# Seven weight chunks' low halves moved from VectorE to GpSimd in the first mixer of a three-layer network

## The reference

```python
def _mixer(u, w_in, ...):
    proj = u @ w_in
    rq, rk, rv, rg, a_cq, a_ckv, a_kr, a_gret, a_gmla = jnp.split(proj, SPLIT_IDX, axis=-1)
    ...
    y_ret = _head_group_norm(_bidir_retention(rq, rk, rv, decay_f, decay_b), gn_w)
    y_ret = (jax.nn.silu(rg) * y_ret) @ w_ret_out
    c_q = _rmsnorm(a_cq, q_norm_w)
    q = (c_q @ w_uq).reshape(B, L, MLA_HEADS, MLA_QK)
    ...
    y_mla = _mla_attention(q_nope, q_rope, k_nope, k_rope, v).reshape(...) @ w_mla_out
    merged = jax.nn.sigmoid(a_gret) * y_ret + jax.nn.sigmoid(a_gmla) * y_mla
    return merged @ w_o
```

## Time and profile before

| | us |
|---|---|
| median of three runs | 1189.4 |
| profiled execution, its own time | 1190.88 |
| span of the profiled execution | 1189.1 |
| TensorE matmul busy | 1128.5 (95% of the span) |
| VectorE busy | 770.1 (65%) |
| ScalarE busy | 514.3 (43%) |
| GpSimd busy | 6.0 (1%) |

### The profile page before, as it was taken

How to read it: one execution, slowest core, us unless ns; L and a number is a source line. 1 busy time by engine, 2 the same in 40 slices (tenths; PEclk the granted TensorE clock), 3 DMA queues, 4 the chain that set the end, 5 groups by cost and what they waited for, 6 DMA issues and landing times.

```text
span 1189.1 us, 21009 instructions
## 1 busy us (share of the span) xinstructions
PE 1128.5 (95%) x8640; PEld 1069.2 (90%) x8640; DVE 770.1 (65%) x860; ACT 514.3 (43%) x512; POOL 6.0 (1%) x6
## 2 busy tenths in 40 slices
PE   8998999799899999998998999999987999999998
PEld 7996777588889999997887999999987999999998
DVE  5765778576756666677755565655479776655563
ACT  5322443334444444446475543333454455434331
POOL 0000001000000000000000000000000000000000
PEclk8998999799999999999998999999989999999999
DMA  9552135034435575672632456554243534554630
GB/s 314 184 159 90 40 115 169 5 121 146 127 105 161 175 208 163 201 239 85 200 107 71 142 181 209 165 188 152 96 150 108 169 107 151 203 192 165 208 106 36
DMA packets 160886, 175.72 MB, mean 148 GB/s; under 512 B 4512, under 2 KB 146848, under 8 KB 160704
## 3 DMA queue, kind: packets, MB, share of 16 engines
q1 hardware_dynamic: 160544, 174.74, 46.3%
q10 hardware_dynamic: 288, 0.21, 0.1%
HBM read 173.89 MB, written 1.05 MB: 147 GB/s over the span
## 4 chain that ended last, share of the span: by engine, by line
PE 76%; DVE 14%; ACT 6%; issue 2%; DMA 0%; SPq 0%; DVEq 0%; ACTq 0%
PE proj L401 46%; PE aux L759 20%; DVE wlo L1373 5%; DVE f L1376 4%; DVE f L1373 2%; ACT whi L1016 2%; PE aux L458 2%; DVE f L1379 1%; PE aux L686 1%; PE aux L669 1%; PE aux L562 1%; PE aux L556 1%; PE aux L679 1%; DMA f<-in_x_dram 0%; DVE x_all L1373 0%
## 5 line engine op out<-in xcount | busy, mean ns | idle before, releaser
L401 PE MATMUL proj<-u,whi 128*128 128x256 f32 (+1 forms) x2912 | 538.3, 286 | 12.5 <-DVE wlo L1373 4.1
L401 PEld LDWEIGHTS proj<-u,whi 128*128 128x128 f32 x2912 | 455.3, 191 | 22.5 <-issue 10.2
L1373 DVE TENSOR_TENSOR wlo<-raw,whi 128x2048 fp32r<-128x2048 f32 (+2 forms) x176 | 374.2, 2126 | 150.4 <-ACT whi L1016 143.3
L401 PE MATMUL proj<-u,wlo 128*128 128x256 f32 (+1 forms) x1456 | 413.6, 284 | 0.0
L1016 ACT ACTIVATE whi<-raw 128x2048 fp32r<-128x2048 f32 (+3 forms) x174 | 311.6, 1791 | 126.9 <-PE proj L401 71.5
L401 PEld LDWEIGHTS proj<-u,wlo 128*128 128x128 f32 x1456 | 278.9, 192 | 0.0
L759 PE MATMUL aux<-v,whi 128*128 128x256 f32 x1376 | 249.9, 283 | 3.0 <-DVE v L1373 3.0
L759 PEld LDWEIGHTS aux<-v,whi 128*128 128x128 f32 x1376 | 214.2, 192 | 3.7 <-issue 3.7
L759 PE MATMUL aux<-v,wlo 128*128 128x256 f32 x688 | 194.6, 283 | 0.0
L759 PEld LDWEIGHTS aux<-v,wlo 128*128 128x128 f32 x688 | 131.9, 192 | 0.0
L401 PE MATMUL proj<-v,whi 128*128 128x256 f32 (+2 forms) x592 | 111.2, 289 | 5.5 <-DVE v L1376 3.1
(11 more groups left out here) (259 smaller groups left out, 787.6 us busy)
## 6 DMA issues: line engine op xcount, KB each, us to landing
raw<-in_mlp_w_dram SPq DMA_DIRECT2D x64, 1024.0 KB, 5.3
raw<-in_w_in_dram SPq DMA_DIRECT2D x21, 1024.0 KB, 5.4
raw<-in_od_w_in_dram SPq DMA_DIRECT2D x12, 1024.0 KB, 5.4
raw<-in_w_ffn_gate_dram SPq DMA_DIRECT2D x22, 512.0 KB, 3.9
raw<-in_w_ffn_up_dram SPq DMA_DIRECT2D x22, 512.0 KB, 5.3
raw<-in_w_ffn_down_dram SPq DMA_DIRECT2D x21, 512.0 KB, 5.4
raw<-in_ev_w_in_dram SPq DMA_DIRECT2D x10, 1024.0 KB, 5.9
raw<-in_w_ret_out_dram SPq DMA_DIRECT2D x4, 1024.0 KB, 5.2
```

Of the source, the lines that this page charges most:

```text
L401: ins = mm(o, w_of(a, k), x_of(b, k), start=first and k == 0 and j == 0, stop=last and k == kt - 1 and j == 2, skip_group_check=skip)
L1373: return ve.tensor_tensor(o, a, b, op)
```

## The change

GpSimd makes the low halves of the chunks in `pool_lo`: rg1, rg3, gm1, gm3 ahead of its two other instructions and ro0, ro2, mo0 behind them. Its `split(n)` waits for all low halves before n and for the high half of n. VectorE leaves these chunks out and counts them as made, and ahead of the next chunk's low half it waits until GpSimd's is there, so that `lo_ready` still rises in the order of the chunks.

```diff
@@ -303,6 +303,7 @@
+        pool_lo = [index[name] for name in ("rg1", "rg3", "gm1", "gm3", "ro0", "ro2", "mo0")]
@@ -1355,11 +1356,23 @@
             G = Lane(eng, sems, "pool_step")
             gp = nc.gpsimd
 
+            def split(n):
+
+                eng.wait_ge(sems["lo_ready"], n)
+                eng.wait_ge(sems["hi_ready"], n + 1)
+                wd, s = width_of(n), n % RING
+                G.here["lo_ready"] = n
+                G.post(gp.tensor_tensor(wlo[:, s, 0:wd], raw[:, s, 0:wd], whi[:, s, 0:wd].bitcast(F32), ALU.subtract), "lo_ready")
+
+            for n in pool_lo[:4]:
+                split(n)
             eng.wait_ge(sems["kr_roped"], 1)
             eng.wait_ge(sems["kv_half"], 1)
             G.post(gp.tensor_copy(k_all[64:96, :, :], bc(kr[64:96, :], 8)), "kr_copied")
             eng.wait_ge(sems["q_mla_rotated"], 2)
             G.post(gp.tensor_tensor(q_pre[0:96], q_pre[0:96], bc(C("cos_mla")[0:96, META:L], 8), ALU.mult), "q_cos")
+            for n in pool_lo[4:]:
+                split(n)
@@ -1380,6 +1393,11 @@
             def split(n, i=None):
 
+                if i is None and n in pool_lo:
+                    B.here["lo_ready"] = B.here.get("lo_ready", 0) + 1
+                    return
+                if i is None and n - 1 in pool_lo:
+                    eng.wait_ge(sems["lo_ready"], n)
                 eng.wait_ge(sems["hi_ready"], at(lambda m: m + 1, n, i))
```

## The result

The changed kernel took 1196.57 us in the median of 20 runs (1191.26 to 1202.08), the kernel before 1189.68 in 20 runs (1187.6 to 1191.95). The ratio is 1.0053, 95% interval 1.0040 to 1.0067: slower by over 0.3%, where 1191.1 us and no change were forecast, and outside the range. Two things stand out: the median is 6.9 us up, but the fastest execution only 3.7; and the executions now spread over 10.8 us, before over 4.4.

The account below looks back on a forecast made before the run. TensorE's matmuls, busy 95% of the span, bound the kernel, so only its waits for VectorE count. Exclusion adds 1.4 + 0.3 = 1.7 us to the 1189.4 us median: 1191.1 us, range 1186.7 to 1194.0.

Parts of the forecast that it names:

- What leaves VectorE: Seven low halves of 2.29 us, 16.0 us of VectorE's time; only chunk 16 was to gain, 1.87 us.
- Chunks 12 and 14: rg1 and rg3: VectorE sat idle behind each low half, so gain 0; with exclusion also cost 0.
- chunk 16: gm1, on the chain: TensorE's waits of 1.18 and 0.69 us would go, gain 1.87; with exclusion 1.4 us cost.
- Exclusion: VectorE's two-SBUF-input instructions and GpSimd's SBUF reads wait for each other's whole length; +1.7 us, chance 0.53.
- the first rival: No exclusion: VectorE and GpSimd run freely side by side, as in an undisturbed pair reading PSUM; 1187.5 us, chance 0.27.
- I take 3.82 for 128x2048: Duration of each GpSimd low half, taken from its own 96x2048 product of 3.82 us.
- the upper bound of 4.6: Longest duration allowed for a GpSimd low half: double VectorE's 2.29 us.
- the sum: Exclusion's cost: 1.4 + 0.3 = +1.7 us; at the duration's upper bound 2.2 + 0.8 + 1.0 + 0.3 = +4.3.
- "Cost 0" for gm3, "0.3" for ro0 and 0 for mo0: Exclusion's costs at chunks 18, 26 and 30, in us; with 4.6 us duration 0.8, 1.0 and 0.3.
- a sign of being wrong: The prediction is wrong if the attention stage shows waits of TensorE that it hadn't.
- a rival with a chance of 0.12: TensorE's clock falls to its lower level behind the wait at 149.49: 4.7 us more, 1195.8 us.
- The wait of 2.6 us: TensorE's wait at 149.49 us, behind chunk 16, grows from 1.18 to 2.6 us with exclusion.

Follow-up runs that it names:

- e3: Only rg1's and rg3's low halves on GpSimd, against the kernel before: 1189.54 us, ratio 1.0003.
- e7: Only gm0's low half on GpSimd, against the kernel before: 1190.96 us, ratio 1.0005.
- e6: Only gm1's low half on GpSimd, started after VectorE's five low parts, against the kernel before: 1189.59 us, ratio 0.9992.
- e9: Kernel before, no GpSimd low halves, VectorE making three low parts twice plus a short one (1.9 us more): 1195.41 us, ratio 1.0053.
- e14: The kernel before with VectorE delayed by 1.9 us, same as e9, run again for a second trace: 1197.48 us.
- e15: The kernel before with VectorE delayed by 1.9 us, same as e9, run again for a third trace: 1191.16 us.
- e2: Only gm1's low half on GpSimd, against the kernel before: 1194.28 us, ratio 1.0043.
- e16: The changed kernel again, unedited, for a trace of a slow execution: 1197.48 us.
- e17: The changed kernel again, unedited, for another trace: 1197.33 us.
- e10: All seven low halves on GpSimd, gm1, ro0 and mo0 held until VectorE's two-SBUF-input instructions are done, against the kernel before: 1195.23 us, ratio 1.0045.
- e8: Kernel before, VectorE making all low halves, GpSimd adding two memsets at gm1's place and two copies at ro0's: 1204.73 us in two runs.

## Why the prediction was wrong

**What leaves VectorE: right.** Chunks 12 and 14 are worth nothing (e3), and gm0, whose place has no neighbour to hold, took both of TensorE's waits away (e7), as was argued for chunk 16. One reading was wrong, without harm: beside chunk 14 VectorE had more than read-outs of PSUM. Two decay arguments took 1.83 us there instead of 0.86, and VectorE sat idle for 1.61 us soon behind them.

**Exclusion: right, over the free pair of the first rival.** The Trainium skill (SBUF — State Buffer, Who interferes with whom) has the rule, and the traces agree: 4.18 us more on five instructions beside a GpSimd instruction of 4.56, none beside memsets (2.60 us), none on a read-out of PSUM (0.69 us in e6).

**The duration: mis-sized.** "I take 3.82 for 128x2048" was the step; it measured 4.56 to 4.78 us. The row came from 96 partitions with one input broadcast over the heads. The Trainium skill's figure (GPSIMD Engine Reference, Elementwise — side-by-side cycle accounting), 4497 ns, was nearer than my row. By the upper bound of 4.6 the sum was +4.3, 3.0 in the heads and 1.3 in attention. The stages show 2.5 in the heads and 1.8 to 3.2 in attention, of which 1.6 are waits for VectorE. So with the right duration the sum was near to what VectorE's delay costs, but it would have put the median at 1193.7, still 2.9 us short.

**"Cost 0" for gm3, "0.3" for ro0 and 0 for mo0** follow from the same step: they measured 0.32, 0.90 and 0.67 us of wait. The last two are the new waits in attention that the prediction had named as a sign of being wrong.

**The clock: the step that failed.** The sum put the clock at nothing and left its fall to a rival with a chance of 0.12, at one place, decided by the length of one wait. That a delay is made larger by the clock was right: a delay of VectorE alone, with no GpSimd, costs 5.5 us in the median where it lengthens the heads' stage by 2 at the full clock, and the eight executions of that kernel (e9, e14, e15) are the longer the lower their mean clock, from 1190.4 us at 0.974 to 1199.5 at 0.966. The working was wrong in three ways:

- The wait of 2.6 us never came. In e2 and e9 VectorE's delay is split over two waits of 1.4 to 1.5 us, one before gm0's first half, since rg2's bank is read out later too. I had looked only at the last wait. In the changed kernel the low clock about rg2's start takes the place of the first of the two, and 1.45 us are left.
- The length of the wait doesn't decide. In e2 and e14 the clock fell behind the waits of 1.4 us, in e9, with the same waits, it didn't. In the trace of the kernel before it falls at 211 us, 12 us behind a wait of 1.87, the last of over 0.25 us before it.
- The fall needn't follow the grown wait at once. In four of five traces of the changed kernel it comes 50 us later, behind that same wait of 1.87 us, which was harmless before.

Against the trace of the kernel before, the two longest traced executions of the changed kernel (e16 and e17) are 6.6 and 6.5 us longer, near the median's 6.9: 2.5 in the heads, 2.1 to 2.3 in the ukv part, 3.0 to 3.2 in attention, 0.9 to 1.1 behind it, less the 2.1 to 2.4 that they are ahead at rg2. This sets them against one execution of the kernel before, so it isn't shown stage by stage what of it is due to the change. What decides in one execution whether the clock falls at a given wait stays open too: like kernels, with like waits, differ (e9 and e14).

**The range** took the scatter of the kernel before for that of the changed one. It grew from a standard deviation of 1.3 us to 2.9 (20 runs each).

## What to carry to other kernels

GpSimd is no spare VectorE: an elementwise instruction of 4.6 us there, itself with two SBUF inputs, stopped VectorE at its next instruction with two SBUF inputs, and at its next `tensor_scalar` with one, so moving 2.3 us of work pays only where VectorE would have been reading PSUM or waiting for that long. Go through what VectorE does in the 4.6 us, down to an instruction of two values. And where TensorE's clock changes between its two levels, a delay can cost more than its length (5.5 us in the median for 2, in e9, one kernel). So measure over many executions and look at their mean clock too, and trust neither a single trace nor the mean clock alone.

## What the runs showed of the hardware

- A VectorE instruction on 128x2 values, 0.17 us alone, took 2.76 us beside GpSimd's product (e10). Reciprocals of 128x256 and 128x272 with one SBUF input took 1.75 and 1.85 us beside it, as in the kernel before (e7).
- GpSimd's memsets of 128x2048, 3.67 us for two, held none of VectorE's five low parts with two SBUF inputs (e8).
- Two executions of one kernel (e9 and e14), with TensorE's two waits at the delayed place alike to 0.05 us, had a mean granted clock of 0.974 and 0.967 and spans of 1188.6 and 1195.7 us. Before the first of these waits the clock had been low from 97 to 100 us in the one and from 102 to 113 us in the other.
